# Second block of a two-block transformer: when the decay gate, the decayed products and the output norm of gated linear attention are computed

## The reference, cut to what matters

```python
log_g = log_sigmoid(g_low @ gla_gate_w + gla_gate_b) / 16
o_b = _gla_chunked(heads(gq, 4), heads(gk, 4), heads(gv, 4), heads(log_g, 4))
o_b = _rmsnorm(o_b, gla_norm_w) * silu(heads(gr, 4))
y_b = o_b.reshape(B, S, GLA_VAL_DIM) @ w_o_gla
g_a = sigmoid(gate_a + b_merge[:D_MODEL]); g_b = sigmoid(gate_b + b_merge[D_MODEL:])
return (g_a * y_a + g_b * y_b) @ w_out
```

## Time and profile before

| | us |
|---|---|
| median of 3 runs | 2639.51 (2639.05 to 2641.15) |
| the profiled execution, its own time | 2638.88 |
| its span in the trace | 2636.9 |
| PE busy in the span | 2557.9 |
| DVE busy | 1573.1 |
| ACT busy | 952.2 |
| POOL busy | 36.7 |

### The profile page before, as it was taken

How to read it: one execution, slowest core, us unless ns; L and a number is a source line. 1 busy time by engine, 2 the same in 40 slices (tenths; PEclk the granted TensorE clock), 3 DMA queues, 4 the chain that set the end, 5 groups by cost and what they waited for, 6 DMA issues and landing times.

```text
span 2636.9 us, 45593 instructions
## 1 busy us (share of the span) xinstructions
PE 2557.9 (97%) x18054; PEld 2005.4 (76%) x18055; DVE 1573.1 (60%) x2952; ACT 952.2 (36%) x1576; POOL 36.7 (1%) x24
## 2 busy tenths in 40 slices
PE   8999999999999999999999979999999999999998
PEld 7998799899899879989988869855555555555553
DVE  7776666777877666577776875534344344334434
ACT  5444554544544455454454534311111111111111
POOL 0000000000000000000000200000000000000000
PEclk9999999999999999999999989999999999999999
DMA  9655335545544543555453325789999999999997
GB/s 284 239 191 216 113 131 224 212 183 191 216 184 177 212 156 144 220 212 188 176 201 130 110 82 192 286 362 425 430 430 430 430 430 430 431 430 430 430 430 302
DMA packets 70924, 704.57 MB, mean 267 GB/s; under 512 B 11063, under 2 KB 11319, under 8 KB 14343
## 3 DMA queue, kind: packets, MB, share of 16 engines
q1 hardware_dynamic: 65736, 695.11, 65.8%
q0 software_dynamic: 5088, 8.05, 1.4%
HBM read 699.43 MB, written 3.67 MB: 267 GB/s over the span
## 4 chain that ended last, share of the span: by engine, by line
PE 77%; DMA 12%; DVE 6%; ACT 3%; issue 1%; SPq 0%; DVEq 0%; ACTq 0%
DMA slot<-in_experts 12%; PE ps L1787 12%; PE ps L1759 10%; PE ps L2321 10%; PE ps L1762 9%; PE ps L1763 9%; PE ps L1790 6%; PE ps L2345 6%; PE ps L2301 5%; PE ps L2358 2%; DVE u_lo L1053 2%; PE ps L1803 1%; PE ps L1807 1%; PE ps L1806 1%; PE ps L2331 1%
## 5 line engine op out<-in xcount | busy, mean ns | idle before, releaser
L1053 DVE TENSOR_TENSOR u_lo<-ring,u_hi 128x1024 fp32r<-128x1024 f32 x500 | 614.5, 1235 | 303.3 <-ACT u_hi L571 296.6
L571 ACT ACTIVATE u_hi<-ring 128x1024 fp32r<-128x1024 f32 x498 | 523.1, 1055 | 396.8 <-PE ps L1759 218.2
L1787 PE MATMUL ps<-hs,u_hi 128*128 128x512 f32 x1408 | 505.4, 401 | 4.0 <-DVE u_lo L1192 1.9
L2321 PE MATMUL ps<-slot,xg 128*64 128x256 f32 x4032 | 460.0, 379 | 5.7 <-DMA slot<-in_experts 5.7
L2321 PEld LDWEIGHTS ps<-slot,xg 128*64 128x64 f32 x4032 | 287.2, 137 | 210.8 <-issue 65.8
L1790 PE MATMUL ps<-hs,u_lo 128*128 128x256 f32 x1408 | 396.2, 281 | 0.0
L1787 PEld LDWEIGHTS ps<-hs,u_hi 128*128 128x128 f32 x1408 | 265.9, 189 | 71.2 <-DVE hs L1079 4.7
L1759 PE MATMUL ps<-hs,u_hi 128*128 128x256 f32 x1000 | 289.6, 290 | 1.9 <-DVE hs L1079 1.2
L1762 PE MATMUL ps<-hs,u_hi 128*128 128x256 f32 x1000 | 285.0, 285 | 0.0
L1763 PE MATMUL ps<-hs,u_lo 128*128 128x256 f32 x1000 | 284.9, 285 | 0.0
L1790 PEld LDWEIGHTS ps<-hs,u_lo 128*128 128x128 f32 x1408 | 267.2, 190 | 0.1
(11 more groups left out here) (379 smaller groups left out, 3604.2 us busy)
## 6 DMA issues: line engine op xcount, KB each, us to landing
slot<-in_experts SPq DMA_DIRECT2D x248, 1536.0 KB, 18.8
ring<-in_stream SPq DMA_DIRECT2D x184, 1536.0 KB, 6.4
extra_in<-in_experts SPq DMA_DIRECT2D x4, 1024.0 KB, 11.9
slot<-in_experts SPq DMA_DIRECT2D x4, 1024.0 KB, 5.0
bias<-bias_rows POOLq DMA_DIRECT2D x2, 1280.0 KB, 11.2
konst<-in_konst POOLq DMA_DIRECT2D x1, 2272.0 KB, 9.2
extra_out<-in_experts SPq DMA_DIRECT2D x4, 512.0 KB, 9.5
slot<-in_experts SPq DMA_DIRECT2D x4, 512.0 KB, 15.1
```

Source lines behind the costliest of these rows:

```text
L571: nc.scalar.activation(u_hi[buffer_of(l, k)][:, :], raw_unit(l, k), ACT.Copy).then_inc(unit_hi, 1)
L1053: nc.vector.tensor_tensor(u_lo[b][:, :], raw, u_hi[b][:, :].bitcast(F32), ALU.subtract).then_inc(unit_lo, 1)
L1787: mm = mm_(ps[:, bank, :], hi[:, b], src[:, c, :, :], start=c == 0, stop=False, skip_group_check=True)
L2321: mm = mm_(ps[h * CAP:(h + 1) * CAP, j % 2, 0:2 * P], xg[:, b, k * PAIRS + c, :], w[:, at:at + 2 * P], start=k == 0 and c == 0, stop=k == ...
```

## The change

The mixer's second half is put in another order, and some operations are replaced.

- The unit of the gate input goes ahead of those of `gqk`. PE enters the heads once five rotation steps are done; the last two stand in DVE's list behind heads 0 and 1.
- The gate's matmuls (`soft_inputs`) run in heads 4 and 6 into bank 5, the bias in DVE's steps 5 and 7, Abs and Exp in halves in ACT's steps 6 and 8, Ln in step 9, ahead of the copy of the last head's output.
- The level without decay comes first, into banks 2 and 3.
- DVE multiplies `expd` into queries and keys with one instruction of 2048 elements (`decayed`), with `expd` broadcast; POOL has no product. Each level's differences are made right behind the product before, `add_level` stands behind the first unit's remainder, and ACT's exponential of the next level behind the first unit.
- Level 0's copy to `off` stands in DVE's list behind the product and differences of level 1; PE's level 1 uses banks 0 and 1 and waits for it.
- The first merge unit is projected before the values are multiplied. ACT squares from PSUM, DVE multiplies silu(gr) into `go` from PSUM in place of the copy. Square roots are taken for two heads at a time, and reciprocal and scaling for one head at a time, each followed by a unit's remainder, while PE works on five merge units.

```diff
-MQK0, GQK0, LOW0, GR0, GV0, SG0, SOUT0 = 8, 24, 32, 33, 41, 49, 81
+MQK0, LOW0, GQK0, GR0, GV0, SG0, SOUT0 = 8, 24, 25, 33, 41, 49, 81
...
+        def level_banks(v):
+            return 2 if v == RAW_LEVEL + 1 else 2 * ((v + 1) % 2)
...
-            for v in range(len(LEVELS) + 1):
-                pool.wait_ge(decay_ready, v + 1)
-                if v > 1:
-                    pool.wait_ge(lev_ready, (v - 2) * TT + 1)
-                pool.tensor_tensor(kd[v % 2][:, :, :], gqk[:, GLA_HEADS:, :],
-                                   expd[:, :].rearrange("p (h t) -> p h t", t=TOK), ALU.mult).then_inc(k_decayed, 1)
...
+                if u in (6, 8):
+                    soft_half((u - 6) // 2)
+                if u == 9:
+                    a.wait_ge(sp_ready, 4)
+                    nc.scalar.activation(gtmp[:, :], gtmp[:, :], ACT.Ln, bias=one_col).then_inc(sp_ready, 1)
...
+            decay(0)
+            for v in range(len(LEVELS)):
+                for n, k in enumerate(GLA_UNITS[v]):
                     after_unit(k)
+                    if n == 0:
+                        decay(v + 1)
...
+            nc.scalar.activation(small[:, 36:37], one_col, ACT.Sqrt)
+            round_unit(L, SG0 + 3)
             for i in range(OUTS):
-                a.wait_ge(go_taken, i + 1)
+                a.wait_ge(go_ready, i + 1)
...
+            root_heads(0)
+            root_heads(1)
+            for i in range(GLA_HEADS):
+                round_unit(L, SG0 + i + 4)
+                round_go(i)
...
+                if u < 2:
+                    rope(6 + u)
+                if u in (5, 7):
+                    i = (u - 5) // 2
+                    v.wait_ge(z_ready, i + 1)
...
+            def decayed(i):
+                v.wait_ge(decay_ready, i + 1)
+                if i > 1:
+                    v.wait_ge(lev_ready, level_count(i - 2))
+                nc.vector.tensor_tensor(qkd[i % 2].rearrange("p (a h) t -> p a (h t)", a=2), gqk.rearrange("p (a h) t -> p a (h t)", a=2),
+                                        expd[:, :].unsqueeze(1).to_broadcast([P, 2, GLA_HEADS * TOK]), ALU.mult).then_inc(qk_decayed, 1)
...
+            differences(0)
+            add_level(RAW_LEVEL + 1)
+            last = len(LEVELS) - 1
+            for i in range(len(LEVELS)):
+                decayed(i)
+                differences(i + 1)
+                for n, k in enumerate(GLA_UNITS[i]):
                     low_unit(L, k + 3)
+                    if n == 0 and i == 1:
+                        v.wait_ge(lev_ready, level_count(0))
+                        nc.vector.tensor_copy(off[:, :, :], ps[:, 0, :].rearrange("p (h t) -> p h t", t=P)).then_inc(lev_taken, 1)
+                    if n == 0 and i > 1:
+                        add_level(i - 1)
+                    if n == 0 and i == last:
+                        decayed(i + 1)
...
-            v.wait_ge(ostd_ready, L + 1)
-            step(nc.vector.reciprocal(rstd[:, :], std[:, :]))
             for i in range(GLA_HEADS):
+                hs_ = slice(i * TOK, (i + 1) * TOK)
+                if i % 2 == 0:
+                    v.wait_ge(ostd_ready, L + i // 2 + 1)
+                step(nc.vector.reciprocal(rstd[:, hs_], std[:, hs_]))
...
+                low_unit(L, SG0 + i + 4)
                 if i > 0:
                     low_go(i - 1)
...
-            pe.wait_ge(roped, HEADS)
...
+                    if u % 2 == 0:
+                        pe.wait_ge(roped, 5 + u // 2)
...
+                else:
+                    pe.wait_ge(lev_taken, 3 if i == 1 else level_count(i - 2) if i > 2 else 2)
+                    level(i, q, k)
+            pe.wait_ge(lev_taken, level_count(len(LEVELS) - 1))
+            gates_and_moba(0, 0)
```

More of the change, by code:

```diff
@@ L200, in build @@
         gr = rest("gr", 10240, DC, TOK)
-        qd = [rest(f"qd{i}", 1024 * i, GLA_HEADS, TOK) for i in range(2)]
-        kd = [rest(f"kd{i}", 2048 + 1024 * i, GLA_HEADS, TOK) for i in range(2)]
+        qkd = [rest(f"qkd{i}", 2048 * i, 2 * GLA_HEADS, TOK) for i in range(2)]
         go = rest("go", 12288, DC, TOK)
@@ L847, in _, with soft_half @@
                 take_pair(4 + p, p % 4, mqk[:, 2 * p:2 * p + 2, :])
-            round_unit(L, GQK0 + 3)
+            round_unit(L, LOW0 + 3)
+            a.wait_ge(proj_ready, L * PROJ + 13)
+            nc.scalar.activation(glow[0:RANK, :], ps[0:RANK, 6, 0:TOK], ACT.Copy).then_inc(proj_taken, 1)
             U0 = L * UNITS
+            def soft_half(i):
+                part = gtmp[:, i * 512:(i + 1) * 512]
+                a.wait_ge(zb_ready, i + 1)
+                nc.scalar.activation(part, lg[:, 2 * i:2 * i + 2, :].rearrange("p h t -> p (h t)"), ACT.Abs).then_inc(sp_ready, 1)
+                a.wait_ge(sp_ready, 2 * i + 1)
+                nc.scalar.activation(part, part, ACT.Exp, scale=-1.0).then_inc(sp_ready, 1)
             def exps2(u):
@@ L868, in _ @@
                     nc.scalar.activation(oas[:, u - 3, 0, :], ps[:, 6 + (u - 3) % 2, 0:TOK], ACT.Copy).then_inc(oa_hi, 1)
-                if u < HEADS and u % 2 == 0:
+                if u < HEADS and u % 2:
                     j = u // 2
[L871 to L874, removed]
+                    take_pair(13 + j, 2 + j % 2, gqk[:, 2 * j:2 * j + 2, :], float(P) ** -0.5 if j < 2 else 1.0)
+                if u in (6, 8):
[3 more added lines that the diff above has]
+                    nc.scalar.activation(gtmp[:, :], gtmp[:, :], ACT.Ln, bias=one_col).then_inc(sp_ready, 1)
             def decay(v):
@@ L1518, in _ @@
+            add_level(last)
+            add_level(last + 1)
+            low_unit(L, SG0 + 3)
             for i in range(OUTS):
-                v.wait_ge(go_ready, i + 1)
-                nc.vector.tensor_copy(go[:, 2 * i:2 * i + 2, :], ps[:, 4 + i, :].rearrange("p (a b) -> p a b", b=TOK)).then_inc(go_taken, 1)
-            for k in range(SG0, SG0 + 6):
-                low_unit(L, k + 3)
+                v.wait_ge(osq_ready, L + i + 1)
+                nc.vector.tensor_tensor(go[:, 2 * i:2 * i + 2, :], ps[:, 4 + i, :].rearrange("p (a b) -> p a b", b=TOK), gr[:, 2 * i:2 * i + 2, :],
+                                        ALU.mult).then_inc(go_taken, 1)
@@ L2142, in _ @@
                     mm_(ps[:, 6 + hd % 2, P:TOK], vs[1], pt[:, 2 * P:3 * P], start=False, stop=True).then_inc(oa_ready, 1)
-            pe.wait_ge(proj_taken, R0 + 17)
-            pe.wait_ge(oa_taken, HEADS)
-            for hh in range(GLA_HEADS):
-                mm = mm_(ps[:, 6 + hh // 2, hh % 2 * TOK:(hh % 2 + 1) * TOK], glaw[:, hh * P:(hh + 1) * P], glow[0:RANK, :], start=True, stop=True)
-            mm.then_inc(z_ready, 1)
             def gate_unit(k):
@@ L2153, in gate_unit @@
                     j, half = divmod(k - GR0, 2)
+                    if half == 0 and j == 1:
+                        pe.wait_ge(zb_ready, 2)
                     if half == 0 and j >= 2:
@@ L2227, in _ @@
                 pe.wait_ge(merged_made, L * DC + m - 1)
-                gates_and_moba(m, SG0 + 4 * m)
+                for part in range(3):
+                    gates_and_moba(m, part)
                 gla_branch(m, SG0 + 4 * m + 3)
-            pe.wait_ge(ostd_ready, L + 1)
+            pe.wait_ge(ostd_ready, L + 2)
             for m in range(DC):
@@ L2577, in lay_out @@
         merge += [ga[m], gb[m], mo[m], gl[m]]
[L2578 removed]
+    units = np.concatenate([by_input(mvw), *(units_of(by_output(w)) for w in (mq, mk, low, gq, gk, grw)), by_input(gvw),
                             np.stack(merge), units_of(by_output(i["w_out_2"][0]))])
```

187 lines of the change are left out of this document (87 added, 100 removed).

## The result

The changed kernel takes 2606.27 us (median of 4 runs, 2605.43 to 2609.66), the kernel before 2639.28 beside it: a ratio of 0.9876 with a 95% interval of 0.9863 to 0.9888, 33.0 us less. The forecast was 2609.0, the range 2602 to 2622.

The account below looks back on a forecast made before the run. The mixer, not the experts' stream, was taken as the bound. The third merge chunk was to come 103.6 us behind the last head instead of 132.2, plus 1.8 from the heads: 30.4 off 2639.51, so 2609 us, range 2602 to 2622.

Parts of the forecast that it names:

- Sum: Whole kernel: third merge chunk 103.6 us behind the last head instead of 132.2, plus 1.8 from the heads: 30.4 us.
- Bound: Whole kernel: experts stream at full DMA rate, the mixer does not; experts end as much earlier as the mixer.
- Rival (c): Behind the mixer: its gain is lost because the experts' stream ends at its own time; 2639 us, chance 0.03.
- Heads: Mixer's heads: entry 3.0 us and clock 1.7 gained, gate matmuls 2.0 and ACT halves 0.9 lost: 1.8 us earlier.
- Gate: Behind H, where PE ends the last head: Ln ends about H + 1.9 us, first product starts at H + 10.9.
- Levels: Decay levels: product 2.3 us, a level every 7.3 to 7.8, DVE and PE ending within a microsecond.
- here it started 0.3 us behind POOL's: Levels of the kernel before: DVE's product took 3.19 us instead of 1.23 because it waited for POOL's.
- Norm: Norm: reciprocal's start to third merge chunk 23.7 us, 22.0 before; PE waits 2 to 3 for the first combine.
- Clock: Slow PE clock: up to 2 us added behind the wait at level 1, 2 us behind the combine's wait.
- Rival (b): Mixer: hand-overs slip, PE's waits leave it at half clock; gain only 15 to 20 us, 2619 to 2624; 0.20.
- Rival (e): Mixer: DVE's and PE's waits shrink where clock losses and hand-overs were added; 2601 to 2604 us, chance 0.12.
- Rival (d): DVE's levels: the 2048-element product runs at the disturbed 6.4 us, 33 us more; 2642 us, chance 0.03.

Follow-up runs that it names:

- a4: Changed kernel with the decay gate (matmuls, bias, Abs, Exp, Ln) made behind the last head, as before: 2609.96 us, ratio 0.9887.
- a3: Changed kernel with PE waiting for all eight rotations ahead of head 0, and rotations 6 and 7 moved ahead in DVE's list: 2611.24 us, ratio 0.9892.
- b1: Changed kernel with each of DVE's eight decayed products done twice, same values: 2627.06 us, ratio 0.9950.
- c1: Kernel before, with only each level's decayed product made one 2048-element DVE operation and POOL's half removed: 2630.83 us, ratio 0.9962.
- a1: Changed kernel with the keys' product back on POOL and DVE's cut to the queries, new order kept: 2606.84 us, ratio 0.9876.
- c2: Changed kernel with the undecayed level last, behind level 7, as before: 2607.28 us, ratio 0.9877.
- b3: Changed kernel with DVE's first merge combine ahead of two units' remainders, and ACT rounding unit 58 between the sigmoid pairs: 2602.94 us, ratio 0.9859.
- b4: Changed kernel with both the first merge combine moved ahead and level 0's copy to `off` one level earlier: 2601.46 us, ratio 0.9853.
- a2: Changed kernel with five merge units' remainders ahead of one 1024-column reciprocal, no unit between the norm's heads: 2617.18 us, ratio 0.9912.
- b2: Changed kernel with level 0's copy to `off` one level earlier in DVE's list: 2606.91 us, ratio 0.9875.

## Why the prediction was right, and where its steps were not

**Sum.** Without the 2 us for the clock behind the combine, which falls outside the stretch, the prediction's terms for the stretch are 132.2 - 101.6 + 1.8 = 32.4 us, and 32.3 were measured. That this is so near is luck: the heads brought 0.7 less, the way from H to the values 1.1 more, from there to the third chunk 0.5 less. Two sums are off as written: 8 x 2.3 is 18.4 and not 18.6, and the norm's 22.0 + 5.8 - 2.4 - 2 is 23.4 and not 23.7.

**Bound.** Right. The experts' stream did not hold the end: 32.3 of the span's 32.5 us come from the stretch in the mixer. Rival (c) is out. The prediction took a longer experts' stretch as a sign of being wrong, and what is behind the third chunk did get 2.7 us longer. But the DMA rate there is the same, and the excess is slow clock of PE behind the combine and at the router, not the stream.

**Heads.** Predicted 1.8 us, measured 1.1 (42.5 to 41.4 from the rotation matmul to H). The entry went as said (head 0 0.97 us after the rotation matmul, full clock); a4 shows the gate's price in the heads as 3.2 where I had 2.0 + 0.9, and a3 the entry's gain there as 4.4 where I had 4.7. Each term was 0.3 off; the last 0.1 I can't place.

**Gate.** First product at H + 10.8, predicted 10.9. Ln ended at H + 1.9 as counted, and its row says again that nothing lies between the table load and the work behind it. This is ACT's timeline of the changed kernel:

```profile
1453.27 1.28 ACT L885 ACT_TABLE_LOAD   x1
1454.56 1.15 ACT L885 ACTIVATE gtmp<-gtmp,konst 128x1024 f32<-128x1024 f32 x1
```

Ln starts 1.29 us after its load began. By the further 1.38 us that the Trainium skill (ScalarE: Activation LUTs, What ACT_TABLE_LOAD costs) counts, it would have started at 1455.9; the row decides for the sum as it was made.

**Levels.** The price was right (2.29 for 2.3), the pace nearly (7.24 for "7.3 to 7.8"), PE's wait at level 1 too (2.46 for 2.8), and DVE and PE end together as said: b1 shows DVE without slack, and PE's rows show no idle time from level 2 on. H to the values took 68.8 us for 69.9. PE was at level 1 at H + 21.5, for 21.4, by luck: the matmuls of level 0 took 1.1 us where I counted a level of 2.0, and PE waited 1.20 for a remainder, which I did not have. What fell is the attribution. I argued the gain of the levels from 3.19 becoming 2.3, and called that the product's doing. It is so in the old order (c1), and in the new one the product is worth nothing (a1). By a1's rows the reason is the new place of the differences and of ACT's exponential, which takes POOL's product out of the way of DVE's by itself. The step that failed is "here it started 0.3 us behind POOL's": I read it as a property of having two products, and it was one of when the exponential comes. The undecayed level's place, which I had as cover for the first exponential and for PE until H + 13.5, is worth nothing either (c2): the cover was there, and four units of projections stood behind it.

**Norm.** From the start of the reciprocal (1530.64) to the third chunk 24.2 us, predicted 23.7; each quarter took 1.75 and not 6.55 / 4 = 1.64, 0.4 in sum. The combine's wait came as predicted, 2.68 in "2 to 3 us". I took it as given; b3 shows it was only an order of two items in two lists.

**Clock.** I added 2 us twice. Behind the wait at level 1 the stretches show 0.74 over 2.5 us of work and 0.92 over 5, about 1.0 us; behind the combine 0.66 over 5 us, about 1.7. So of the 4 us that I allowed 2.7 were spent. The forecast was 2.7 us too high, and 1.3 of that lie here; the rest can't be placed, since the start of the stretch alone scatters by 3 us and the clock at the router by up to 5. Rival (b) needed long waits to make slow stretches of 10 to 15 us; none of the waits passed 2.7. Rival (e) was nearer than (b): two waits stood between the changed kernel and it, b3, which removes one of them, lands at 2602.94, and b4 without both at 2601.46.

**Rival (d).** The product ran at 2.29 in every level. Its theory would have been right on the price: b1 asks 19.7 us for 8 x 2.29.

**Open.** Undone one at a time, the parts are worth 7.6 us (the meeting of DVE and POOL, c1), 3.8 (the entry, a3), 2.2 (the gate, a4) and 10.3 (the norm, a2): 23.9 of the 32.3, if they add, which a1 and c1 show that they need not. The other 8.4 are not traced to a part by a run. Rows of the kernel before show waits that are gone in the changed one: DVE's for the exponential in levels 0 to 2 (1.13, 1.12 and 0.53) and this one of PE:

```profile
1534.59 3.76 PE L2184 MATMUL ps<-qd,kd 128*128 128x128 f32 x16 [6.04 <-DVE qd L1512]
```

## What to carry to other kernels

An effect that two parts of a change can each bring must be tested in both orders: undoing one part of the new kernel said "worth nothing", doing it alone in the old one said 9.5 us, and both are true. Where two engines are both full, taking away a wait of one moves it to the end of the stretch; look first for a wait behind which nobody else is late, such as a consumer queued behind two items that are not ready. When a DVE operation with two SBUF inputs shows two or three times its usual duration, look at what POOL does at that moment, and before merging the work see whether one of the two can be set beside something that reads PSUM.

## What the runs showed of the hardware that I had not expected

- Beside a POOL product of 2.41 us DVE's masked copies from PSUM kept their 1.52, while the remainder (two SBUF inputs) behind them took 2.06 for 1.22. Before, DVE's product took 3.19 for 1.23.
- A reciprocal of 256 columns takes 1.75 us, four of them 7.0; one of 1024 took 6.55.
- The clock behind a wait of one length is not always the same. The combine's wait of 2.68 us was followed by 0.66 over 5 us in the changed kernel; in b2 and c2 it stands at 2.67 and 2.68 and is followed by 1.00, while in c2 the two short waits of 1.13 and 1.27 ahead of level 1 are followed by 0.66. These are the stretches of c2:

```profile
1470.00:1475.00 5.00, 4.18 (x24) 4.21 (x25) 4.07 (x4) 3.95 (x5) 0.00 (x0) 0.66 0.24 57
...
1555.00:1560.00 5.00, 3.48 (x29) 3.48 (x30) 4.02 (x8) 1.66 (x3) 0.00 (x0) 1.00 0.72 258
```

  Each such stretch is worth 1 to 2 us, so a difference of that size between two profiles is no evidence for an edit unless the rows show where it comes from. What decides whether the clock falls is left open.
